# Cross attention by heads, placed between the halves of the query projection's tiles

## The chip, the cores and the metric

The kernel runs on one core of a Trainium2 chip. The metric is device time in microseconds (us) for one execution of the whole program. The kernel before the change takes 1310.12 us (median of three runs, 1309.95 to 1310.24).

Engines are named as in the profile: PE is TensorE (matmuls; PEld are its weight loads), ACT is ScalarE, DVE is VectorE, POOL is GpSimd, SP is SyncE, which issues the DMAs.

## The reference

Two transformer blocks in a row on 512 tokens of width 1024, all in float32. The part that the change touches is the first block's cross attention to a memory of 256 rows, with 4 heads of 256:

```python
def memory_cross_attention(x, mem, wq, wkv, wo):
    q = (x @ wq).reshape(B, S, XA_HEADS, XA_HEAD_DIM)          # S = 512, 4 heads of 256
    k, v = jnp.split(mem @ wkv, 2, axis=-1)                    # M = 256
    ...
    logits = jnp.einsum('bshd,bmhd->bhsm', q, k) * (XA_HEAD_DIM ** -0.5)
    p = jax.nn.softmax(logits, axis=-1)
    o = jnp.einsum('bhsm,bmhd->bshd', p, v).reshape(B, S, D_MODEL)
    return o @ wo
```

Ahead of it stand a mixer (an mLSTM and a sliding-window attention) with a layer norm, and behind it a layer norm, a convolutional feed-forward, and the second block (four mixers, a projection, an MLP).

## The kernel before

**Precision.** Every large product is made of three products of split floats: weights and activations are each held as a high part (`whi`, `xh`) and a low part (`wlo`, `xl`), and PE multiplies high by high, high by low and low by high (L1097 to L1099 where the weights are the stationary operand, L1206 to L1211 where the activations are). The weights come as chunks of 128 x 1024 by DMA into a ring of three `stage` buffers. For each chunk the step `split` casts it on ACT (L1455) and subtracts on DVE (L1870) into a ring of six `whi`/`wlo` buffers. The small products of the attentions are plain float32 matmuls, each shown as two records.

**Order of work.** The class `Plan` writes one list of steps by hand. Each engine walks through this list and executes, in this order, the steps for which it has a function of that name; between engines there are only semaphores. Each engine's own queue is strict. PSUM has eight banks of 128 x 512; `fill` takes the bank that was released first and `out` puts it back with the semaphore value that makes it free. `pump` adds splits so that six chunks are ahead of the one in use.

**Query projection.** `cross_attention` runs `feat("xq", 8)`: eight tiles of 128 features x 512 tokens, 24 matmuls each. Tiles 0 to 3 have their first 256 tokens done already at the end of the layer norm before (`half`), so that only `feat_rest` with 256 tokens is left. ACT copies every tile, scaled by 1/16, into `qT` (L1623).

**Attention, by token tiles of 128.** For token tile i, with all four heads: PE makes the scores of two heads at a time into one bank (`xa_score`, L1365, after all eight query tiles are out); DVE takes the negated row maximum (L2130); ACT makes exp and the row sums into `Lx` (L1632); DVE takes reciprocals (L2135) and multiplies the 128 x 1024 tile (`xa_norm`, L2137); PE turns it in two banks (`xa_turn`, L1373), and ACT copies them into `PTx` (L1637). `Lx` has two buffers. The order is scores 0, scores 1, turn 0, scores 2, turn 1, scores 3, turn 2, turn 3. Then come `decay`, a chain of small operations on parameters of the second block (DVE L2144 to L2171, ACT L1641), and the value product: eight feature tiles k of 512 tokens (`xa_pv`, L1381), each split by ACT (L1646) and DVE (L2175) into `xh` and `xl`, which the output projection "xo" reads.

**An existing helper.** `feat_mid(name, n, mid)` is like `feat`, but cuts each tile's 24 matmuls into a front and a back half and calls `mid()` between them; it does not do so for a tile of which only `feat_rest` is left (but for "in2_a"). The mixers use it: a generator such as `beside_mixer_one` is advanced by one `yield` at each call of `mid`.

Of the kernel before, what the change touches and what calls it, by code (L numbers as in the profile page):

```python
# [47 lines left out]
class Plan:  # L48
# [482 lines left out]

    def cross_attention(self):
        for k in self.feat("xq", 8):
            self.step("xq", k)
            self.out(("xq", k), "q_out", k + 1)

        def scores(i):
            for hp in range(2):
                self.fill("xa_score", i, hp)
                self.step("xa_score", i, hp)  # L540
                self.out(("xa_score", i, hp), "xa_e", 4 * i + 2 * hp + 2)
            self.step("xa_norm", i)

        scores(0)
        for i in range(4):
            if i < 3:
                scores(i + 1)
            for m in range(2):
                self.fill("xa_turn", i, m)
                self.step("xa_turn", i, m)  # L550
                self.out(("xa_turn", i, m), "xa_pt", 2 * i + m + 1)
        self.step("decay")
        for k in range(8):
            self.fill("xa_pv", k)
            self.step("xa_pv", k)
            self.x_split("xo", k)
            self.out(("xa_pv", k), "x_lo", self.x)
        self.step("rows", "ln2")
        self.tok_full("xo", 8, 8)
        self.step("warm", 1)  # L560
        self.boundary("xo", 8, lambda t: self.norm("xo", 1, t))
# [359 lines left out]
def build_program(nc, d, out):  # L921
    plan = Plan()
    with ExitStack() as ctx:
# [26 lines left out]
        def tiles(view, n):  # L950
            return view.rearrange("p (k c) -> p k c", k=n)
# [105 lines left out]
        def tok(t):  # L1057
            return slice(t * 128, (t + 1) * 128)
# [23 lines left out]
        def _(e):  # L1082
            q = Waits(e)

            def fill(*key):

                b, left = plan.bank[key]
                if left:
                    q.wait_ge(S[left[0]], left[1])
                return bank[b]  # L1090
# [267 lines left out]
            def xa_score(i, hp):  # L1358
                b = tiles(fill("xa_score", i, hp)[:], 2)
                q.wait_ge(S["q_out"], 8)  # L1360
                q.wait_ge(S["kt_out"], 8)
                for hh in range(2):
                    h = 2 * hp + hh
                    for kk in range(2):
                        last = e.matmul(b[:, hh, :], qT[:, 2 * h + kk, tok(i)], KT[:, 2 * h + kk, :], start=(kk == 0),  # L1365
                                        stop=(kk == 1))
                last.then_inc(S["xa_s_full"])

            def xa_turn(i, m):
                b = fill("xa_turn", i, m)  # L1370
                q.wait_ge(S["xa_p"], i + 1)
                for h in range(4):
                    last = e.transpose(b[:, tok(h)], Lx[i % 2][:, h, tok(m)], ident[:])  # L1373
                last.then_inc(S["xa_t_full"])

            def xa_pv(k):
                b = fill("xa_pv", k)
                q.wait_ge(S["xa_pt"], 8)
                q.wait_ge(S["vm_out"], 4)
                for m in range(2):  # L1380
                    last = e.matmul(b[:], VM[:, m, tok(k)], PTx[:, m, k // 2, :], start=(m == 0), stop=(m == 1))  # L1381
                last.then_inc(S["xa_o_full"])
# [63 lines left out]
        def _(e):  # L1446
# [178 lines left out]
            def xa_score(i, hp):  # L1625
                b = tiles(bank_of("xa_score", i, hp)[:], 2)
                if i >= 2:
                    q.wait_ge(S["xa_t_full"], 2 * i - 2)
                q.wait_ge(S["xa_m"], 2 * i + hp + 1)
                for hh in range(2):  # L1630
                    h = 2 * hp + hh
                    e.activation(Lx[i % 2][:, h, :], b[:, hh, :], ACT.Exp, bias=lx(i, 1)[:, h:h + 1],  # L1632
                                 accum_out=lx(i, 2)[:, h:h + 1]).then_inc(S["xa_e"])

            def xa_turn(i, m):
                q.wait_ge(S["xa_t_full"], 2 * i + m + 1)
                e.copy(PTx[:, m, :, tok(i)], tiles(bank_of("xa_turn", i, m)[:], 4)).then_inc(S["xa_pt"])  # L1637
# [201 lines left out]
            def m1(k):  # L1839
# [6 lines left out]
                        warm=warm, layer_norm=layer_norm, xq=xq, xa_score=xa_score, xa_turn=xa_turn, decay=decay,  # L1846
# [10 lines left out]
        def _(e):  # L1857
# [270 lines left out]
            def xa_score(i, hp):  # L2128
                q.wait_ge(S["xa_s_full"], 2 * i + hp + 1)
                e.tensor_reduce(lx(i, 1)[:, 2 * hp:2 * hp + 2], tiles(bank_of("xa_score", i, hp)[:], 2), AX.X, ALU.max,  # L2130
                                negate=True).then_inc(S["xa_m"])

            def xa_norm(i):
                q.wait_ge(S["xa_e"], 4 * i + 4)
                e.reciprocal(lx(i, 0), lx(i, 2)).then_inc(own.inc())  # L2135
                after()
                e.tensor_tensor(Lx[i % 2], Lx[i % 2],  # L2137
                                lx(i, 0).rearrange("p (h c) -> p h c", c=1).to_broadcast([128, 4, 256]), ALU.mult
                                ).then_inc(S["xa_p"])
# [474 lines left out]
```

## Time and profile before

| | us |
|---|---|
| median of three runs | 1310.12 |
| the profiled execution | 1310.3 |
| its span | 1308.5 |
| PE busy | 1289.0 |
| DVE busy | 721.7 |
| ACT busy | 556.5 |

The span is the time from the first to the last recorded instruction; the rest of the execution's own time lies around it. The busy times of the engines overlap. In a timeline each row gives start and length in us, the engine, the line of the kernel, the operation, its operands and the number of instructions merged into the row; the brackets give idle time of the engine before the row and what ended it. Starts of consecutive matmuls are closer together than their lengths, since they are pipelined and their ends are modelled.

### The profile page before, as it was taken

The page shows a single profiled execution, that of the slowest core. Times are in us where ns is not written, and L with a number is a line of the kernel's source. Part 1 is how long each engine was busy: PE and PEld are TensorE (multiplying, and loading weights), DVE is VectorE, ACT ScalarE, POOL GpSimd, SP SyncE. Part 2 cuts the span into 40 slices and gives each one's busy share as a digit, 9 for nine tenths or more (in the row PEclk, how much of TensorE's full clock was granted, in tenths as well). Part 3 has the DMA queues.
Part 4 walks back from the last instruction along what each step waited for, and adds up shares of the span by engine and source line. Part 5 has one row for each costly group of instructions (what it writes and reads, how often), then busy time and mean ns, then how long its engine had stood idle before and what let it go on. Part 6 is the DMA issues. An engine that isn't in the chain of part 4 may idle for free.

```text
span 1308.5 us, 16066 instructions
## 1 busy us (share of the span) xinstructions
PE 1289.0 (99%) x6504; PEld 1074.8 (82%) x6504; DVE 721.7 (55%) x1060; ACT 556.5 (43%) x944; POOL 7.0 (1%) x8
## 2 busy tenths in 40 slices
PE   8999999999899999999999989999999999999998
PEld 8877898898589888888888889777898888888886
DVE  5757678563457655555633478877473333433333
ACT  4567644144315544444422354576332422322221
POOL 0000001000000000000000000000000000000000
PEclk9999999999899999999999999999999999999999
DMA  8322245333013333333433123222243233333311
GB/s 271 117 80 65 97 129 160 129 126 117 1 49 104 115 99 97 98 97 100 145 97 97 49 89 125 81 66 88 73 136 95 92 103 98 118 97 100 95 51 65
DMA packets 37714, 131.22 MB, mean 100 GB/s; under 512 B 4324, under 2 KB 5092, under 8 KB 37384
## 3 DMA queue, kind: packets, MB, share of 16 engines
q1 hardware_dynamic: 37640, 130.19, 31.7%
q8 instruction: 52, 0.85, 0.3%
q14 instruction: 22, 0.18, 0.0%
HBM read 128.07 MB, written 2.10 MB: 99 GB/s over the span
## 4 chain that ended last, share of the span: by engine, by line
PE 96%; DVE 1%; ACT 1%; issue 0%; DMA 0%; DVEq 0%; ACTq 0%
PE bank L1097 17%; PE bank L1098 17%; PE bank L1099 17%; PE bank L1206 5%; PE bank L1207 5%; PE bank L1210 5%; PE bank L1209 5%; PE bank L1208 5%; PE bank L1211 5%; PE bank L1381 1%; PE bank L1271 1%; PE bank L1137 1%; PE bank L1148 1%; PE bank L1142 1%; PE bank L1348 1%; PE bank L1334 1%
## 5 line engine op out<-in xcount | busy, mean ns | idle before, releaser
L1097 PE MATMUL bank<-xh,whi 128*128 128x512 f32 (+1 forms) x1168 | 421.8, 361 | 4.1 <-DVE wlo L1870 4.1
L1870 DVE TENSOR_TENSOR wlo<-stage,whi 128x1024 fp32r<-128x1024 f32 (+1 forms) x223 | 268.4, 1209 | 276.0 <-ACT whi L1455 275.8
L1098 PE MATMUL bank<-xl,whi 128*128 128x512 f32 (+1 forms) x1168 | 415.7, 356 | 0.0
L1099 PE MATMUL bank<-xh,wlo 128*128 128x512 f32 (+1 forms) x1168 | 415.5, 356 | 0.0
L1455 ACT CAST whi<-stage 128x1024 fp32r<-128x1024 f32 (+1 forms) x223 | 229.4, 1034 | 216.1 <-PE bank L1211 170.0
L1097 PEld LDWEIGHTS bank<-xh,whi 128*128 128x128 f32 x1168 | 220.6, 189 | 43.2 <-issue 9.3
L1099 PEld LDWEIGHTS bank<-xh,wlo 128*128 128x128 f32 x1168 | 220.6, 189 | 31.5
L1098 PEld LDWEIGHTS bank<-xl,whi 128*128 128x128 f32 x1168 | 220.8, 189 | 30.9 <-issue 0.7
L1206 PE MATMUL bank<-whi,xh 128*128 128x512 f32 x287 | 113.0, 394 | 0.2
L1208 PE MATMUL bank<-wlo,xh 128*128 128x512 f32 x287 | 111.7, 389 | 0.0
L1207 PE MATMUL bank<-whi,xh 128*128 128x512 f32 x287 | 111.7, 389 | 0.0
L1211 PE MATMUL bank<-whi,xl 128*128 128x512 f32 x287 | 111.7, 389 | 0.0
L1209 PE MATMUL bank<-wlo,xh 128*128 128x512 f32 x287 | 111.7, 389 | 0.0
L1210 PE MATMUL bank<-whi,xl 128*128 128x512 f32 x287 | 111.7, 389 | 0.0
L2378 DVE TENSOR_TENSOR R<-bank,R 128x512 f32<-128x512 f32 x32 | 22.1, 692 | 90.5 <-ACT R L1841 90.5
L1841 ACT ACTIVATE R<-bank 128x512 f32<-128x512 f32 x32 | 19.1, 598 | 112.8 <-PE bank L1099 112.8
L2189 DVE SCALAR_TENSOR_TENSOR R<-R,par 128x512 f32<-128x512 f32 x44 | 33.1, 751 | 60.3 <-ACT R L1657 60.3
L1206 PEld LDWEIGHTS bank<-whi,xh 128*128 128x128 f32 x287 | 53.9, 188 | 12.1 <-issue 1.3
L1209 PEld LDWEIGHTS bank<-wlo,xh 128*128 128x128 f32 x287 | 53.9, 188 | 11.3
L1211 PEld LDWEIGHTS bank<-whi,xl 128*128 128x128 f32 x287 | 53.9, 188 | 11.3
L1208 PEld LDWEIGHTS bank<-wlo,xh 128*128 128x128 f32 x287 | 53.9, 188 | 11.3
L1210 PEld LDWEIGHTS bank<-whi,xl 128*128 128x128 f32 x287 | 53.9, 188 | 11.1
(311 smaller groups left out, 1310.1 us busy)
## 6 DMA issues: line engine op xcount, KB each, us to landing
stage<-in_W_m SPq DMA_DIRECT2D x64, 512.0 KB, 3.6
stage<-in_W_up SPq DMA_DIRECT2D x44, 512.0 KB, 3.6
stage<-in_W_down SPq DMA_DIRECT2D x22, 512.0 KB, 3.6
stage<-in_W_in_a SPq DMA_DIRECT2D x19, 512.0 KB, 3.7
stage<-in_W_out SPq DMA_DIRECT2D x16, 512.0 KB, 3.7
stage<-in_W_in_b SPq DMA_DIRECT2D x10, 512.0 KB, 3.7
stage<-in_W_kv_k SPq DMA_DIRECT2D x8, 512.0 KB, 3.6
stage<-in_W_kv_v SPq DMA_DIRECT2D x8, 512.0 KB, 4.1
```

The lines of the kernel that those rows point to most:

```text
L1097: e.matmul(b[:, cols], hi[:, k, :], xh[:, k, cols], start=(k == 0), stop=False)
L1098: e.matmul(b[:, cols], hi[:, k, :], xl[:, k, cols], start=False, stop=False)
L1099: last = e.matmul(b[:, cols], lo[:, k, :], xh[:, k, cols], start=False, stop=(k == 7))
L1206: e.matmul(b[0][:], a_hi, hi[:, 0:512], start=(k == 0), stop=False)
L1207: e.matmul(b[1][:], a_hi, hi[:, 512:1024], start=(k == 0), stop=False)
L1208: e.matmul(b[0][:], a_hi, lo[:, 0:512], start=False, stop=False)
L1209: e.matmul(b[1][:], a_hi, lo[:, 512:1024], start=False, stop=False)
L1210: e.matmul(b[0][:], a_lo, hi[:, 0:512], start=False, stop=end)
L1211: return e.matmul(b[1][:], a_lo, hi[:, 512:1024], start=False, stop=end)
L1455: e.copy(whi[:, i % NSPLIT, 0:width(i)], stage[:, s, 0:width(i)]).then_inc(S["w_hi"])
L1870: e.tensor_tensor(wlo[:, i % NSPLIT, c], stage[:, i % NSTAGE, c], whi[:, i % NSPLIT, c].bitcast(F32), ALU.subtract).then_inc(S["w_lo"])
L2189: e.scalar_tensor_tensor(out=y, in0=u[:, 0:512], scalar=P("fcw", w), in1=y, op0=ALU.mult, op1=ALU.add).then_inc(own.inc())
```

## The change

The attention is cut by heads. For head h, with all four token tiles: `xa_score(h)` makes the scores in two banks of two token tiles, as soon as the query tiles 2h and 2h+1 are out; `xa_exp(h)`, a step of its own now, makes the four exponentials; `xa_norm(h)` multiplies; `xa_turn(h)` turns the four token tiles of this head in two banks, whose copies each fill one whole row of `PTx`; `xa_pv(k)` waits only for its own head k // 2.

The order is a generator, `beside_queries`, advanced by `feat_mid` in the middle of query tiles 4 to 7 and after each of the eight tiles. What is left of it when the queries are done follows then. `decay` moves behind the last `xa_pv`.

```diff
             self.out((name, 2 * t + hf), "ln_z", 8 * s + 2 * t + hf + 1)
 
+    def xa_score(self, h):
+        for z in range(2):
+            self.fill("xa_score", h, z)
+            self.out(("xa_score", h, z), "xa_e", 4 * h + 2 * z + 2)
+        self.step("xa_score", h)
+
+    def xa_turn(self, h):
+        for m in range(2):
+            self.fill("xa_turn", h, m)
+            self.out(("xa_turn", h, m), "xa_pt", 2 * h + m + 1)
+        self.step("xa_turn", h)
+
+    def xa_pv(self, k):
+        self.fill("xa_pv", k)
+        self.step("xa_pv", k)
+        self.x_split("xo", k)
+        self.out(("xa_pv", k), "x_lo", self.x)
+
+    def beside_queries(self):
+
+
+        yield
+        yield
+
+        self.xa_score(0)
+        yield
+
+        self.step("xa_exp", 0)
+        yield
+
+        self.step("xa_norm", 0)
+        self.xa_score(1)
+        yield
+        self.step("xa_exp", 1)
+        yield
+
+        self.xa_turn(0)
+        yield
+        self.step("xa_norm", 1)
+        yield
+
+        self.xa_score(2)
+        yield
+        self.xa_turn(1)
+        self.step("xa_exp", 2)
+        yield
+
+        self.step("xa_norm", 2)
+        yield
+        yield
+        self.xa_pv(0)
+        self.xa_score(3)
+        self.step("xa_exp", 3)
+        self.xa_turn(2)
+        self.step("xa_norm", 3)
+        self.xa_pv(1)
+        self.xa_pv(2)
+        self.xa_pv(3)
+        self.xa_turn(3)
+        self.xa_pv(4)
+        self.xa_pv(5)
+        self.xa_pv(6)
+        self.xa_pv(7)
+        self.step("decay")
+
     def cross_attention(self):
-        for k in self.feat("xq", 8):
+        side = self.beside_queries()
+
+        def mid():
+            next(side, None)
+
+        for k in self.feat_mid("xq", 8, mid):
             self.step("xq", k)
             self.out(("xq", k), "q_out", k + 1)
-
-        def scores(i):
-            for hp in range(2):
-                self.fill("xa_score", i, hp)
-                self.step("xa_score", i, hp)
-                self.out(("xa_score", i, hp), "xa_e", 4 * i + 2 * hp + 2)
-            self.step("xa_norm", i)
-
-        scores(0)
-        for i in range(4):
-            if i < 3:
-                scores(i + 1)
-            for m in range(2):
-                self.fill("xa_turn", i, m)
-                self.step("xa_turn", i, m)
-                self.out(("xa_turn", i, m), "xa_pt", 2 * i + m + 1)
-        self.step("decay")
-        for k in range(8):
-            self.fill("xa_pv", k)
-            self.step("xa_pv", k)
-            self.x_split("xo", k)
-            self.out(("xa_pv", k), "x_lo", self.x)
+            mid()
+        for _ in side:
+            pass
         self.step("rows", "ln2")
         self.tok_full("xo", 8, 8)
...
-            def xa_score(i, hp):
-                b = tiles(fill("xa_score", i, hp)[:], 2)
-                q.wait_ge(S["q_out"], 8)
+            def xa_score(h):
+                q.wait_ge(S["q_out"], 2 * h + 2)
                 q.wait_ge(S["kt_out"], 8)
-                for hh in range(2):
-                    h = 2 * hp + hh
-                    for kk in range(2):
-                        last = e.matmul(b[:, hh, :], qT[:, 2 * h + kk, tok(i)], KT[:, 2 * h + kk, :], start=(kk == 0),
-                                        stop=(kk == 1))
-                last.then_inc(S["xa_s_full"])
-
-            def xa_turn(i, m):
-                b = fill("xa_turn", i, m)
-                q.wait_ge(S["xa_p"], i + 1)
-                for h in range(4):
-                    last = e.transpose(b[:, tok(h)], Lx[i % 2][:, h, tok(m)], ident[:])
-                last.then_inc(S["xa_t_full"])
+                for z in range(2):
+                    b = tiles(fill("xa_score", h, z)[:], 2)
+                    for i in range(2):
+                        for kk in range(2):
+                            last = e.matmul(b[:, i, :], qT[:, 2 * h + kk, tok(2 * z + i)], KT[:, 2 * h + kk, :],
+                                            start=(kk == 0), stop=(kk == 1))
+                    last.then_inc(S["xa_s_full"])
+
+            def xa_turn(h):
+                q.wait_ge(S["xa_p"], h + 1)
+                for m in range(2):
+                    b = fill("xa_turn", h, m)
+                    for i in range(4):
+                        last = e.transpose(b[:, tok(i)], Lx[h % 2][:, i, tok(m)], ident[:])
+                    last.then_inc(S["xa_t_full"])
 
             def xa_pv(k):
                 b = fill("xa_pv", k)
-                q.wait_ge(S["xa_pt"], 8)
+                h = k // 2
+                q.wait_ge(S["xa_pt"], 2 * h + 2)
                 q.wait_ge(S["vm_out"], 4)
                 for m in range(2):
-                    last = e.matmul(b[:], VM[:, m, tok(k)], PTx[:, m, k // 2, :], start=(m == 0), stop=(m == 1))
+                    last = e.matmul(b[:], VM[:, m, tok(k)], PTx[:, m, h, :], start=(m == 0), stop=(m == 1))
                 last.then_inc(S["xa_o_full"])
...
-            def xa_score(i, hp):
-                b = tiles(bank_of("xa_score", i, hp)[:], 2)
-                if i >= 2:
-                    q.wait_ge(S["xa_t_full"], 2 * i - 2)
-                q.wait_ge(S["xa_m"], 2 * i + hp + 1)
-                for hh in range(2):
-                    h = 2 * hp + hh
-                    e.activation(Lx[i % 2][:, h, :], b[:, hh, :], ACT.Exp, bias=lx(i, 1)[:, h:h + 1],
-                                 accum_out=lx(i, 2)[:, h:h + 1]).then_inc(S["xa_e"])
-
-            def xa_turn(i, m):
-                q.wait_ge(S["xa_t_full"], 2 * i + m + 1)
-                e.copy(PTx[:, m, :, tok(i)], tiles(bank_of("xa_turn", i, m)[:], 4)).then_inc(S["xa_pt"])
+            def xa_exp(h):
+                if h >= 2:
+                    q.wait_ge(S["xa_t_full"], 2 * h - 2)
+                for z in range(2):
+                    b = tiles(bank_of("xa_score", h, z)[:], 2)
+                    q.wait_ge(S["xa_m"], 2 * h + z + 1)
+                    for i in range(2):
+                        t = 2 * z + i
+                        e.activation(Lx[h % 2][:, t, :], b[:, i, :], ACT.Exp, bias=lx(h, 1)[:, t:t + 1],
+                                     accum_out=lx(h, 2)[:, t:t + 1]).then_inc(S["xa_e"])
+
+            def xa_turn(h):
+                for m in range(2):
+                    q.wait_ge(S["xa_t_full"], 2 * h + m + 1)
+                    e.copy(PTx[:, m, h, :], bank_of("xa_turn", h, m)[:]).then_inc(S["xa_pt"])
```

The counts of instructions and the names of the semaphores stay; the DVE functions `xa_score(h)` and `xa_norm(h)` have the same change of index (token tile to head) as those shown.

## Rows read from the trace of the kernel before

**Rows 1.** The page: busy time, the clock in 40 slices.

```profile
PE 1289.0 (99%) x6504; PEld 1074.8 (82%) x6504; DVE 721.7 (55%) x1060; ACT 556.5 (43%) x944; POOL 7.0 (1%) x8
...
PEclk9999999999899999999999999999999999999999
```

**Rows 2.** Windows: length, busy PE, PEld, DVE, ACT, POOL, granted clock, DMA.

```profile
280.00:314.00 34.00, 33.52 (x194) 29.41 (x193) 8.93 (x8) 11.19 (x15) 0.00 (x0) 1.00 0.41 136
328.00:330.00 2.00, 2.00 (x11) 1.71 (x10) 1.89 (x3) 0.86 (x3) 0.00 (x0) 1.00 0.00 0
332.00:334.00 2.00, 0.42 (x3) 0.45 (x4) 1.84 (x7) 0.93 (x2) 0.00 (x0) 0.93 0.00 0
334.00:336.00 2.00, 1.39 (x7) 0.99 (x5) 0.00 (x0) 1.16 (x3) 0.00 (x0) 0.50 0.00 0
...
340.00:342.00 2.00, 2.00 (x5) 0.77 (x5) 1.53 (x7) 0.54 (x1) 0.00 (x0) 0.86 0.00 0
```

**Rows 3.** Timeline of PE in the stage: start, duration, line, operands, count, idle before.

```profile
312.45 0.39 PE L1099 MATMUL bank<-xh,wlo 128*128 128x512 f32 x1
...
313.13 0.39 PE L1099 MATMUL bank<-xh,wlo 128*128 128x512 f32 x1
314.30 7.14 PE L1365 MATMUL bank<-R 128*128 128x256 f32 x32 [0.78 <-ACT R L1623]
321.30 1.09 PE L1373 MATMUL bank<-ident,R 128*128 128x128 f32 x8
...
325.68 1.04 PE L1373 MATMUL bank<-ident,R 128*128 128x128 f32 x8
326.56 3.62 PE L1365 MATMUL bank<-R 128*128 128x256 f32 x16
330.01 1.04 PE L1373 MATMUL bank<-ident,R 128*128 128x128 f32 x8
333.58 1.82 PE L1373 MATMUL bank<-ident,R 128*128 128x128 f32 x8 [2.53 <-DVE R L2137]
336.16 16.15 PE L1381 MATMUL bank<-R 128*128 128x512 f32 x32 [0.77 <-ACT R L1637]
...
352.38 0.39 PE L1207 MATMUL bank<-whi,xh 128*128 128x512 f32 x1
```

**Rows 4.** Timeline of ACT in the stage.

```profile
313.55 0.60 ACT L1623 ACTIVATE R<-bank 128x512 f32<-128x512 f32 x1 [3.91 <-PE bank L1099]
...
335.43 0.59 ACT L1637 COPY R<-bank 128x512 f32<-128x512 f32 x1 [0.27 <-PE bank L1373]
...
342.05 0.59 ACT L1646 CAST xh<-bank 128x512 fp32r<-128x512 f32 x1 [1.51 <-PE bank L1381]
...
352.35 0.59 ACT L1646 CAST xh<-bank 128x512 fp32r<-128x512 f32 x1 [1.13 <-PE bank L1381]
```

**Rows 5.** Groups of ACT from 290 to 345: count, busy us, mean ns, idle before.

```profile
L1632 ACT ACTIVATE R<-bank,st 128x256 f32<-128x256 f32 x16 | 7.4, 471 | 5.7 <-DVE st L2130 5.7
...
L1632 ACT ACT_TABLE_LOAD x1 | 1.3, 1283 | 0.0
```

**Rows 6.** Timeline of DVE at the last score and in decay.

```profile
332.21 1.22 DVE L2137 TENSOR_TENSOR R<-R,st 128x1024 f32<-128x1024 f32 x1
...
340.94 0.17 DVE L2171 TENSOR_SCALAR par<-par 128x2 f32<-128x2 f32 x1
```

**Rows 7.** Timeline of PE at two groups between split-float matmuls.

```profile
197.00 2.32 PE L1334 MATMUL bank<-R 128*128 128x512 f32 x8
198.97 0.59 PE L1185 MATMUL bank<-whi,xh 128*128 128x512 f32 x1
199.40 0.40 PE L1186 MATMUL bank<-wlo,xh 128*128 128x512 f32 x1
...
276.31 1.04 PE L1271 MATMUL bank<-ident,R 128*128 128x128 f32 x8
...
277.30 0.28 PE L1098 MATMUL bank<-xl,whi 128*128 128x256 f32 x1
```

More of the change, by code:

```diff
@@ L1845, in _ @@
                         conv_qk=conv_qk, silu_qk=silu_qk, in_o=in_o, ml_exp=ml_exp, kv_k=kv_k, kv_v=kv_v,
-                        warm=warm, layer_norm=layer_norm, xq=xq, xa_score=xa_score, xa_turn=xa_turn, decay=decay,
+                        warm=warm, layer_norm=layer_norm, xq=xq, xa_exp=xa_exp, xa_turn=xa_turn, decay=decay,
                         xa_pv=xa_pv, up=up, rms_stats=rms_stats, rms_late=rms_late, ln_apply=ln_apply, last_norm=last_norm, cf_in=cf_in, cf_first=cf_first, cf_mean=cf_mean,
@@ L2126, in ln_apply, with xa_score, xa_norm @@
                                        op1=ALU.add).then_inc(S["ln_x"])
[L2128 to L2135, printed above, removed]
+            def xa_score(h):
+                for z in range(2):
+                    q.wait_ge(S["xa_s_full"], 2 * h + z + 1)
+                    e.tensor_reduce(lx(h, 1)[:, 2 * z:2 * z + 2], tiles(bank_of("xa_score", h, z)[:], 2), AX.X, ALU.max,
+                                    negate=True).then_inc(S["xa_m"])
+            def xa_norm(h):
+                q.wait_ge(S["xa_e"], 4 * h + 4)
+                e.reciprocal(lx(h, 0), lx(h, 2)).then_inc(own.inc())
                 after()
-                e.tensor_tensor(Lx[i % 2], Lx[i % 2],
-                                lx(i, 0).rearrange("p (h c) -> p h c", c=1).to_broadcast([128, 4, 256]), ALU.mult
+                e.tensor_tensor(Lx[h % 2], Lx[h % 2],
+                                lx(h, 0).rearrange("p (t c) -> p t c", c=1).to_broadcast([128, 4, 256]), ALU.mult
                                 ).then_inc(S["xa_p"])
```

## The prediction

> **What bounds the kernel now.** I read the page's busy table and clock line first [rows 1]. TensorE (PE) is busy for 1289.0 of 1308.5 us, 99%. So a stage is worth only what PE loses in it. The clock line has one digit under 9, at about 335 us. The windows of that place [rows 2] show the granted clock at 1.00 (2.4 GHz) in 328 to 330 and at 0.50 (1.2 GHz) in 334 to 336. Read as shares of the two levels, 0.93 in 332 to 334 puts the fall at 333.7, and 0.86 in 340 to 342 the return at 340.6. That place is the cross attention.
>
> PE's own order of work [rows 3] gives the stage. The queries' matmuls step every 0.227 us (313.13 - 312.45 for three), the last starting at 313.13, so the next could start at 313.36. The first matmul of the output projection that runs in step starts at 352.38, which puts the end of attention at 352.15. The stage takes 352.15 - 313.36 = 38.79 us.
>
> What would it take without waits, at 2.4 GHz? Sixteen score records take 330.01 - 326.56 = 3.45 us, and there are four such groups: 13.80. Eight transposes take 326.56 - 325.68 = 0.88, four groups: 3.52. Once the clock is back, the value product's tiles reach ScalarE (ACT) every (352.35 - 342.05) / 6 = 1.717 us [rows 4]; eight: 13.73. The sum is 31.05, so 7.74 us are lost, as follows.
> - 0.94: the scores wait for ACT's copy of the last query tile (313.36 to 314.30).
> - 0.10: the first 32 score records take 7.00 and not 6.90.
> - 2.69: the last group of turns could start at 330.89 and starts at 333.58. Behind the last score stands a chain: maximum on VectorE (DVE), two exponentials on ACT, reciprocal and product on DVE [rows 6]. From the last score to the first transpose it takes 333.58 - 330.01 = 3.57.
> - 1.70: most of these transposes run at 1.2 GHz, and the value product waits for ACT's second copy of them (started 335.43 [rows 4]); 336.16 instead of 334.46.
> - 2.26: the value product takes 352.15 - 336.16 = 15.99 instead of 13.73, since it runs at 1.2 GHz until 340.6: half of 4.4 us.
>
> **The change part by part.** *Amount of work.* By heads or by token tiles, PE has the same 32 score products of 256 columns, 32 transposes and 16 value products of 512 columns; ACT has the same 16 exponentials and 8 copies, DVE the same 8 maxima and 4 products of 1024. The copy of the turned tile now writes a row in one piece instead of four; the one of before takes 0.59 us [rows 4] and PSUM is read the same, so I cost it at nothing. No DMA is added or moved.
>
> *Places.* The query tiles 0 to 3 run as second halves of 256 columns, without a middle; tiles 4 to 7 have one. That gives 4 + 8 = 12 places for the 12 pieces of the new generator, which fit exactly: scores of head 0 after tile 2; of head 1 and 2 in the middle of tiles 4 and 6; turns of head 0 in the middle of 5, of head 1 after 6. Only pv 0, scores 3, turns 2, pv 1 to 3, turns 3 and pv 4 to 7 come after the queries.
>
> *The switch between kinds of matmul.* This is new: three score groups and two turn groups now stand between the split-float matmuls, and each could cost PE something. In mixer one a group of such products already stands so [rows 7]: from 197.00 to the second split-float matmul at 199.40 is 2.40 us; its 1280 columns at the score's rate (3.45 / 2048 per column) are 2.16, and one step is 0.227: 0.02 is left. Eight transposes between halves: 277.30 - 276.31 - 0.12 = 0.87, the 0.88 of the stage. The other end: if the long step after the group (199.40 - 198.97 = 0.43) were a cost by itself and not the group's own last columns, it would be 0.20. So 5 x 0 to 5 x 0.20; I take 0.2 for all five, near the whole-group figures, which count every column.
>
> *The waits of PE, one by one*, with T the end of tile 7. Scores of head h need tiles 2h and 2h+1 on ACT. ACT starts such a copy 0.2 us after the tile and takes 0.60 [rows 4]; scores 0 to 2 have a tile or a half tile (2.72 us) between. Scores 3 follow T directly, but pv 0 stands before them: 1.72 against about 0.85, 0.87 spare. Turns 0 need the chain from scores 0: I get product 0 done some 4 us before they are reached (the wait in it is DVE's subtraction of a weight chunk, queued before it); turns 1 have over 8 us. Turns 2, reached at T + 5.17, need product 2, which stands after the exponentials 2 and one weight chunk, about T + 1.4: 3.8 spare. Turns 3 are the tight ones. Scores 3 end at T + 1.72 + 3.45 = T + 5.17; by the 3.57 of the chain the transposes could start at T + 8.74. PE has turns 2 (0.88) and pv 1 to 3 (5.15) until T + 11.20: 2.46 spare. Behind turns 3 queue pv 4 to 7 and the whole output projection. pv 6 needs their copies (about T + 13.1) and is reached at T + 15.5. Banks go round in the order of release; I followed them through and each fill finds its bank free by over a microsecond.
>
> *The cover.* What was in the open must fit on ACT and DVE beside the queries and the weight splits. From 280 to 314 ACT is busy for 11.2 of 34 us and DVE for 8.9 [rows 2]. Until T come three heads' exponentials (12 at 0.47 [rows 5]), two pairs of copies (1.1 each) and the table load (1.28): about 9; DVE gets six maxima (about 0.7) and three products of 1.22 with a reciprocal each [rows 6]: about 8.3. Neither passes two thirds, and weight chunks are split six ahead. If this cover fails, the first to show it would be turns 3, one for one after its 2.46 us.
>
> *Decay.* Its chain of small DVE operations ran from the last product's end at 333.43 to 341.11 [rows 6], 7.7 us; it now stands behind pv 7's subtraction, beside the output projection, and ends at most 9.7 us into it. Behind it on DVE is the split of the next weight chunk, which waits for the projection's first chunk (24 steps, 5.4 us) and ACT's cast. It may be late by some 3 us; that chunk is the projection's seventh, used after three whole chunks and three quarters of a chunk, 20.4 us in. SyncE's queue issues the later weights a little later by the same amount; nothing.
>
> *The clock.* With no wait of PE over a microsecond left, nothing resembles what came before the fall at 333.7 (0.94, then 2.69 us idle). So 1.00 throughout.
>
> *Sum.* The new stage is 31.05 + 0.2 = 31.25; 38.79 - 31.25 = 7.54. I keep 0.15 back for small delays at semaphores: gain 7.4. The profiled execution took 1310.3 us (span 1308.5); it becomes 1302.9. The median of the three runs is 1310.12, 0.18 below, so the forecast is 1302.7.
>
> **The rivals.** (a) *Some of it leaks.* At the eight insertions or in the tail small waits stay, 0.1 to 0.5 each, because ACT's copy of a query tile comes behind exponentials, or because each return from the queries' copy to the exponentials loads the table again (1.28). For it: ACT and DVE are strict queues, and three kinds of work now meet there. Against it: the sixteen exponentials of before, with copies of turned tiles between them, have one load in all [rows 5], and the groups in mixer one start without idle time before them [rows 7]. Eight times 0.35: 1305.5.
> (b) *The wait moves to turns 3.* A chain of 3.57 would have to become over 8 us, as it must pass the weight split of ACT and DVE and pv 0's copies first. Then 2.69 idle and the half clock behind it come back, and only the 0.94, the 0.10 and the 0.8 inside 1.70 are won, less 0.2: 1310.1 - 1.6 = 1308.5, which is no change by the bound below. Against it: those passages end before scores 3 do.
> (c) *The clock falls inside the queries; slower than before.* Place: the groups of transposes between halves. If they ended the full clock, PE would run at 1.2 GHz for as long after each as it did here, 6.9 us, which costs half of that, 3.4. Four groups: 13.7, against 7.4 won: 1310.1 + 6.3 = 1316.4. It decides from the third such fall. Against it: the transposes at 325.68 are followed by scores at full rate [rows 3], with the windows of 328 to 330 at 1.00 [rows 2].
> The Trainium skill bears on (c): "TensorE: Matmul & The Clock Gate", Part 4 on transposes, says that the full clock does not engage for the transpose mode. By that rule alone (c) would be likely, and the time 1316.4. The trace disagrees for groups of eight: the clock stays, and they take 0.88 us at 1.00 against 1.82 at 0.50.
> (d) *It doesn't do what it says.* The generator is drained after the queries too, so pieces that found no place would run there with today's waits: 1310. The count of 12 places excludes it.
>
> **How the numbers follow.** Forecast 80%, (a) 12%, (b) 4%, (c) 3%, (d) 1%. The forecast's own spread is 1302.3 (switches free, nothing kept back) to 1303.5 (switches at 1.0). The range reaches into (a): 1302.0 to 1305.6. A difference under 0.2% (2.6 us) is what a measurement here can't tell from none. Faster: forecast and (a), 92%; same: (b) and (d), 5%; slower: 3%.
>
> **What would show it.** In the profile after: the clock line without a low digit; one query tile's distance 5.44 us plus the group in it (8.9 with scores, 6.3 with turns); the output projection's first step near 344.7 instead of 352.15; turns 3 without idle time before them, their product on DVE ending about 2 us earlier; decay beside the projection. Wrong would be: idle time of PE before a score or turn group, a second table load, or a granted clock under 1.00 anywhere between 280 and 350 us.

## The result, and the profile after

The changed kernel takes 1304.4 us (median of four runs, 1301.88 to 1304.76) against 1310.18 for the kernel before: ratio 0.9949, 95% interval 0.9936 to 0.9961. The forecast was 1302.7, in a range of 1302.0 to 1305.6. On a second chip the same kernel took 1302.69 against 1310.33 (first experiment below). The profiled execution took 1304.55 us, its span 1302.8.

The page of the kernel after, its busy table and clock line, which answer to [rows 1]:

```profile
PE 1287.3 (99%) x6504; PEld 1075.6 (83%) x6504; DVE 721.6 (55%) x1060; ACT 556.1 (43%) x944; POOL 7.0 (1%) x8
...
PEclk9999999999999999999999999999999999999999
```

The digit under 9 at 335 us is gone. (A digit is the mean of a fortieth of the span, 32.6 us, so a shorter fall need not show in it; one stands below.) The windows (length, busy PE, PEld, DVE, ACT, POOL, granted clock, DMA) answer to [rows 2] in their first lines:

```profile
280.00:314.00 34.00, 34.00 (x205) 30.68 (x205) 13.30 (x15) 15.20 (x31) 0.00 (x0) 1.00 0.37 109
334.00:336.00 2.00, 2.00 (x6) 0.84 (x5) 1.29 (x2) 0.89 (x3) 0.00 (x0) 1.00 0.56 221
766.00:768.00 2.00, 0.18 (x2) 0.00 (x0) 0.75 (x1) 2.00 (x4) 0.00 (x0) 1.00 0.00 0
768.00:770.00 2.00, 1.47 (x8) 1.47 (x9) 1.96 (x5) 1.06 (x2) 0.00 (x0) 0.76 0.44 47
770.00:772.00 2.00, 2.00 (x11) 2.00 (x11) 2.00 (x2) 0.00 (x0) 0.00 (x0) 0.50 0.54 215
772.00:774.00 2.00, 2.00 (x18) 2.00 (x18) 0.20 (x1) 0.32 (x1) 0.00 (x0) 0.89 0.40 98
```

From 280 to 314 ACT is busy for 15.2 us and not 11.2, DVE for 13.3 and not 8.9: the exponentials and products of heads 0 and 1 and the copies of head 0's turns lie in this stretch (head 2's exponentials follow at 321.32, still ahead of the end of tile 7), and PE is busy for all 34.0. At 334 the clock is at 1.00. But the last four lines show something that the profile of the kernel before does not: PE is almost idle from 766 to 768.5, and the clock is at 0.50 (1.2 GHz) right behind it. The timeline of PE (start, length, line, operands, count, idle time before) answers to [rows 3] and [rows 7]:

```profile
289.18 3.62 PE L1416 MATMUL bank<-R 128*128 128x256 f32 x16
292.45 0.47 PE L1148 MATMUL bank<-xh,whi 128*128 128x256 f32 x1
292.75 0.28 PE L1149 MATMUL bank<-xl,whi 128*128 128x256 f32 x1
...
307.17 1.03 PE L1425 MATMUL bank<-ident,R 128*128 128x128 f32 x8
...
308.27 0.40 PE L1149 MATMUL bank<-xl,whi 128*128 128x512 f32 x1
...
326.01 1.88 PE L1434 MATMUL bank<-R 128*128 128x512 f32 x4
327.73 3.62 PE L1416 MATMUL bank<-R 128*128 128x256 f32 x16
331.18 1.04 PE L1425 MATMUL bank<-ident,R 128*128 128x128 f32 x8
...
337.21 1.04 PE L1425 MATMUL bank<-ident,R 128*128 128x128 f32 x8
...
345.19 0.40 PE L1258 MATMUL bank<-whi,xh 128*128 128x512 f32 x1
```

No row of the stage has idle time before it. Tile 7 ends at 326.01 (T), the last turns start at 337.21, which is the forecast T + 11.20, and the projection is in step at 345.19, so attention ends at 344.96. To compare the stages whatever came before them, I take the start of query tile 3 or of the group placed before it: 288.69 in the kernel before, 289.18 here. From there to the end of attention it was 352.15 - 288.69 = 63.46 us and is 344.96 - 289.18 = 55.78: 7.68 won, 7.54 by the sum, 7.4 in the forecast.

The spans differ by 5.7. The other 2.0 are 0.49 lost before the stage and 1.5 lost behind it. For the second, this is PE at the wait for the fourth weight chunk of the second block's projection, before:

```profile
775.72 0.39 PE L1097 MATMUL bank<-xh,whi 128*128 128x256 f32 x1 [2.35 <-DVE wlo L1870]
...
776.18 0.29 PE L1097 MATMUL bank<-xh,whi 128*128 128x256 f32 x1
776.30 0.28 PE L1098 MATMUL bank<-xl,whi 128*128 128x256 f32 x1
```

and after:

```profile
768.53 0.39 PE L1148 MATMUL bank<-xh,whi 128*128 128x256 f32 x1 [2.35 <-DVE wlo L1925]
...
769.15 0.42 PE L1149 MATMUL bank<-xl,whi 128*128 128x256 f32 x1
769.37 0.41 PE L1150 MATMUL bank<-xh,wlo 128*128 128x256 f32 x1
```

The wait is the same, 2.35 us for the same DVE subtraction. Before, the matmuls of 256 columns go on at 0.12 us apart; after, at 0.21. The window behind the wait shows the full clock before:

```profile
776.00:778.00 2.00, 2.00 (x19) 2.00 (x19) 1.97 (x4) 0.25 (x1) 0.00 (x0) 1.00 0.60 193
```

The first matmul behind the wait starts 7.19 earlier than before, those behind the slow stretch 5.7. The 0.49 comes from the start of the kernel, where the first eight matmuls take 2.3 us to the next ones in all three profiles shown now. Here are before, after, and a third kernel (the experiment "filler"), each in one line:

```profile
9.53 1.35 PE L1148 MATMUL bank<-whi,xl 128*128 128x264 f32 x8
```

```profile
9.59 2.12 PE L1199 MATMUL bank<-whi,xl 128*128 128x264 f32 x8
```

```profile
9.09 1.34 PE L1203 MATMUL bank<-whi,xl 128*128 128x264 f32 x8
```

Before and in "filler" this third group is at its later pace already; after, it takes 2.12 us. The kernels are equal here, so it is the execution that differs. The clock column of the windows reads 1.00 here, but this is no evidence: the profile's clock record begins only at 9.46 us before, 11.27 after and 8.54 in "filler", at the full clock, and that is where each changes its pace. So the slow start fits the half clock, and no row shows it as such. By the fourth group the kernel after is 0.83 behind; up to 33.5 us its groups then start 1.18 us apart against 1.20 before, which gives 0.34 back. Why they do stays open.

### The profile page after: what moved, and what is told of

Same layout as the page of the kernel before. It is cut to its first block, busy times and chain, and to the rows that moved or that the text cites. A ratio compares the mean times of both kernels' runs of the same rounds, so it can differ in the third digit from the quotient of the medians.

```text
span 1302.8 us, 16066 instructions
## 1 busy us (share of the span) xinstructions
PE 1287.3 (99%) x6504; PEld 1075.6 (83%) x6504; DVE 721.6 (55%) x1060; ACT 556.1 (43%) x944; POOL 7.0 (1%) x8
## 4 chain that ended last, share of the span: by engine, by line
PE 98%; DVE 1%; ACT 1%; issue 0%; DMA 0%; DVEq 0%; ACTq 0%
PE bank L1148 18%; PE bank L1149 17%; PE bank L1150 17%; PE bank L1257 5%; PE bank L1259 5%; PE bank L1262 5%; PE bank L1258 5%; PE bank L1260 5%; PE bank L1261 5%; PE bank L1416 1%; PE bank L1434 1%; PE bank L1322 1%; PE bank L1188 1%; PE bank L1199 1%; PE bank L1193 1%; PE bank L1399 1%
## 5 line engine op out<-in xcount | busy, mean ns | idle before, releaser
L1259 PEld LDWEIGHTS bank<-wlo,xh 128*128 128x128 f32 x287 | 53.9, 188 | 11.2
L1260 PEld LDWEIGHTS bank<-wlo,xh 128*128 128x128 f32 x287 | 53.9, 188 | 11.2
L1262 PEld LDWEIGHTS bank<-whi,xl 128*128 128x128 f32 x287 | 53.9, 188 | 11.2
```

Of the source, the lines that this page charges most:

```text
L1259: e.matmul(b[0][:], a_hi, lo[:, 0:512], start=False, stop=False)
L1260: e.matmul(b[1][:], a_hi, lo[:, 512:1024], start=False, stop=False)
L1262: return e.matmul(b[1][:], a_lo, hi[:, 512:1024], start=False, stop=end)
```

## The experiments

All times are medians; the kernel before ran beside each of them on the same chip. T1 is my theory, T2 the rival, as in the expectations.

**The changed kernel again.** No edit.

> The changed kernel once more, to see how its times spread. Theory (T1): the attention stage always wins about 7.7 us; at 766 us TensorE waits 2.35 us for a weight chunk, and whether the clock falls behind that wait differs from execution to execution, so times fall into groups: 1304.3 to 1304.8 with the fall, about 1302 without, the first more often. Rival (T2): something in the new kernel always costs 1.5 us after the stage, then all runs lie within 0.5 us of 1304.5 and the one at 1301.9 was chance.

Measured: 1302.69 us (1302.21 to 1303.77, five runs) against 1310.33: ratio 0.9939 (0.9926 to 0.9953). The profiled run, at 1303.77 the slowest, has the fall again, behind the same wait. The spread is there, T2's fixed 1304.5 is not. The times alone do not form the two clear groups of T1, but the mean granted clock, which is on record for each run, parts them. In the thirteen profiled executions of this document it is 0.999 or 1.000 where the clock falls nowhere ahead of the last microseconds (eight of them), 0.998 in the three with one short fall like this one, and 0.997 in the two with the longer fall of [rows 2]. By it four of the nine timed runs of the changed kernel have a fall: three of the first four, at 1304.25 to 1304.76, and the slowest here, at 1303.77. The other five have 0.999 or 1.000 and take 1301.88 to 1302.95.

```profile
766.00:768.00 2.00, 0.19 (x1) 0.19 (x2) 1.47 (x2) 2.00 (x4) 0.00 (x0) 0.92 0.00 0
768.00:770.00 2.00, 2.00 (x10) 2.00 (x11) 1.97 (x4) 0.34 (x1) 0.00 (x0) 0.50 0.55 160
770.00:772.00 2.00, 2.00 (x15) 2.00 (x15) 1.48 (x2) 0.00 (x0) 0.00 (x0) 0.73 0.25 102
```

**The same order by heads, nothing beside the queries ("drain").**

```diff
-        for k in self.feat_mid("xq", 8, mid):
+        for k in self.feat("xq", 8):
             self.step("xq", k)
             self.out(("xq", k), "q_out", k + 1)
-            mid()
```

> By heads, but nothing placed beside the queries: all pieces follow after query tile 7, in the same order. If the placement brings the gain (T2), the stage is near the 38.8 us of before and the time near 1310. If the order by heads brings it, since value products of finished heads stand where TensorE waited for the last turns (T1), only the 0.94 us wait for the last query copy comes back and perhaps 0.2 at the first turns: stage 31.9 to 32.4 us, clock 1.00, time 0.5 to 1.2 us above the changed kernel where both have or both lack the fall at 770.

Measured: 1304.32 (1302.73 to 1305.02) against 1310.33, ratio 0.9952 (0.9939 to 0.9964). PE's timeline after the queries:

```profile
312.90 7.07 PE L1415 MATMUL bank<-R 128*128 128x256 f32 x32
320.40 1.09 PE L1424 MATMUL bank<-ident,R 128*128 128x128 f32 x8 [0.44 <-DVE R L2192]
...
336.86 1.04 PE L1424 MATMUL bank<-ident,R 128*128 128x128 f32 x8
...
344.83 0.39 PE L1257 MATMUL bank<-whi,xh 128*128 128x512 f32 x1
```

The stage takes 344.60 - 312.90 = 31.70 us; without its 0.44 of idle time at the first turns it would be where the changed kernel is. The 0.94 wait that I had expected here is gone too: the scores of head 0 need only tiles 0 and 1. So T2 falls: of 7.68 us, 7.1 come with the order by heads. In time the kernel lies further above the changed one than the 0.5 to 1.2 expected: 1.6 by the medians, and 1.2 to 1.4 where both have or both lack the fall by their mean clock. By the stages 0.6 of it is explained: 31.70 against 55.78 less 24.67 us for five query tiles, 31.11, in the changed kernel.

**Value products behind the last turns ("turn_first").**

```diff
+        self.xa_turn(3)
         self.xa_pv(1)
         self.xa_pv(2)
         self.xa_pv(3)
-        self.xa_turn(3)
```

> The changed kernel with value products 1 to 3 moved from ahead of the last turns to behind them; the places beside the queries stay. T1 (the order by heads is what hides the last softmax, because these 5.15 us of products stand in front of the last turns): TensorE reaches the turns 0.88 us after the last scores, the chain needs 3.6, so a wait of 2.5 to 2.8 us comes back at the turns, with or without a fall of the clock behind it: 2.7 us above the changed kernel without, 4.4 to 6 with. T2 (the placement beside the queries hides it): under 0.5 us above.

Measured: 1307.13 (1306.21 to 1309.29) against 1310.71, ratio 0.9975 (0.9965 to 0.9984). On the scale of ratios that is 3.4 to 4.7 us above the changed kernel (0.9949 and 0.9939), at the low end of or below the 4.4 to 6 expected with a fall; the mean clock, 0.998 or 0.997, says that all ten runs have at least one. Its PE and its windows:

```profile
334.37 1.37 PE L1425 MATMUL bank<-ident,R 128*128 128x128 f32 x8 [2.43 <-DVE R L2193]
```

```profile
334.00:336.00 2.00, 1.63 (x9) 1.51 (x10) 0.31 (x1) 0.81 (x2) 0.00 (x0) 0.76 0.42 170
336.00:338.00 2.00, 2.00 (x3) 0.67 (x2) 0.00 (x0) 0.36 (x1) 0.00 (x0) 0.50 0.00 0
```

The wait is back at the turns with 2.43 us of idle time, though five groups of PE still lie beside the queries (three of scores, two of turns), and the clock falls behind it. What hides the last softmax is the 5.15 us of value products.

**Matmuls in the later wait ("filler").**

```diff
+                if (name, j) == ("in2_c", 3):
+                    old = w_of(CHUNK0[name] + j - 1, 8)[0]
+                    for z in range(18):
+                        e.matmul(bank_of(name, j)[:, 0:256], old[:, z % 8, :], xh[:, z % 8, 0:256], start=True, stop=True)
```

> The changed kernel with 18 more matmuls of 256 columns (0.12 us each, 2.15 in all, their result overwritten) on TensorE in the 2.35 us wait for the fourth weight chunk of the second block's first projection, at 766 us. T1: the wait is filled, the clock stays at 1.00 there, the 1.5 us of half rate go; no other time changes: 1302.7 to 1303.2, with less spread than the changed kernel. T2 (the clock falls for another reason, or the loss lies elsewhere): the fall at 769 stays and the time is 1304.4 or up to 0.3 more.

Measured: 1302.49 (1301.79 to 1303.09) against 1310.33, ratio 0.9939 (0.9926 to 0.9951). Its clock shows no fall at all in the profile; but the kernel without the filler had come to 1302.69 on this chip, so the medians do not show a gain. Its best run is 0.4 below the other's best, its slowest 0.7 below the other's slowest. The mean clocks say why: only one of that kernel's five runs had a fall to lose. They also decide for T1. With the 2.35 us wait in place (the changed kernel, drain and, below, shift) eight of nineteen runs have 0.998; with the order by heads and without this wait (filler, early_split, both_splits, both_again, both_drain) none of twenty-three has.

**The cause of the later wait ("early_split").** The weight split that PE waits for stood behind the last RMS statistics on ACT, which themselves waited 2.82 us for DVE:

```profile
764.74 1.06 ACT L1733 ACTIVATE R<-R 128x1024 f32<-128x1024 f32 x1 [2.82 <-DVE R L2180]
```

```diff
         self.pump(1)
-        norm(3)
-        self.half(name, 1)
+        self.step("ln_apply", 3)
         self.pump(1)
+        self.step("rms_stats", 3)
+        self.half(name, 1)
```

> The changed kernel with the cause of that wait taken away: the split of the fourth weight chunk is placed ahead of the last RMS statistics and not behind them; ScalarE idles 2.8 us there. T1: the 2.35 us wait shrinks to under 0.3 and the clock does not fall: 1304.4 - 2.1 - 1.5 = 1300.8 where the changed kernel has the fall, 1300.3 to 1301.2. Rival: DVE passes the wait on to the last RMS product, and turns 3 then wait: 1302.5 to 1304.

Measured: 1300.85 (1300.14 to 1301.11) against 1310.33, ratio 0.9925 (0.9913 to 0.9937). It is 1.8 below the changed kernel of the same chip, four of whose five runs had no fall to lose, and the spread falls from 1.6 us to 1.0. PE's waits there, the kernel above first:

```profile
PE bank L1148 <- DVE wlo L1925: 4.1, 2, 2.3
```

```profile
PE bank L1149 <- DVE wlo L1926: 1.7, 1, 1.7
PE bank L1323 <- DVE R L2268: 0.4, 1, 0.4
```

Two waits of 4.1 in total become one of 1.7, and 0.4 reach turns 3: about a sixth of the gain ends where the rival said.

**The same edit in the kernel before ("before_split").**

> The kernel before, with only the split of the fourth weight chunk placed ahead of the last RMS statistics. T1: the wait at the second block's first projection and the clock behind it are no part of the change, so the old kernel wins by this edit what the changed one won, 1.9 us (1.3 to 2.5): ratio to before 0.9985. T2 (the change brought that loss with it): 0 to 0.5 us.

Measured: 1308.52 (1305.08 to 1309.4, eleven runs) against 1310.71, ratio 0.998 (0.9971 to 0.9989): 2.2 us by the medians (2.6 by the ratio). The wait belongs to both kernels; T2 falls. Whether the clock falls behind it in the kernel before too is not shown: the one profile there is has no fall at that place, and the waits that the edit takes away in the trace, 2.35 less a new one of 0.4, account for most of the gain. Two of the eleven runs lie apart, 1305.08 and 1305.27, with a mean clock of 0.999 against 0.996 or 0.997 in the other nine, and the first of them is the profiled one. Its PE and its windows in the attention:

```profile
329.39 1.04 PE L1374 MATMUL bank<-ident,R 128*128 128x128 f32 x8
332.95 1.07 PE L1374 MATMUL bank<-ident,R 128*128 128x128 f32 x8 [2.52 <-DVE R L2138]
334.83 13.97 PE L1382 MATMUL bank<-R 128*128 128x512 f32 x32 [0.82 <-ACT R L1638]
...
348.87 0.39 PE L1208 MATMUL bank<-whi,xh 128*128 128x512 f32 x1
```

```profile
332.00:334.00 2.00, 1.05 (x8) 0.86 (x8) 1.25 (x6) 0.68 (x2) 0.00 (x0) 1.00 0.00 0
334.00:336.00 2.00, 1.18 (x4) 0.68 (x4) 0.99 (x6) 0.79 (x3) 0.00 (x0) 1.00 0.00 0
336.00:338.00 2.00, 2.00 (x6) 0.85 (x5) 1.65 (x10) 0.58 (x1) 0.00 (x0) 1.00 0.03 8
```

These are the waits of [rows 3] to 0.05 us, and the clock stays at 1.00. The stage takes 348.64 - 312.73 = 35.91 us, not 38.79. So of the 7.74 us that the attention lost, 4.86 are waits and slow sequences of their own, and 2.88 are the clock, which falls in most executions and not in all. Here `decay` still stands ahead of the value product, which takes 348.64 - 334.83 = 13.81 us against 13.73 for the same tiles in step; so of the gain by the new order at most 0.1 can come from moving `decay`, which no experiment moved by itself.

**Both later waits ("both_splits").** The changed kernel with early_split's edit and this one:

```diff
-        norm(2)
+        self.step("ln_apply", 2)
         self.step("tail", name, nk, 3, "front")
+        self.used += 3
+        self.pump(1)
         self.turn(name, 1)
+        self.step("rms_stats", 2)
         self.step("tail", name, nk, 3, "back")
-        self.used += TAIL[name]
+        self.used += TAIL[name] - 3
         self.pump(1)
         self.step("rms_apply", 2)
-        self.pump(1)
```

> The changed kernel with the early split of the fourth chunk and also the first chunk's split placed ahead of the third RMS statistics, where ScalarE idles 3.6 us. T1: the 1.7 us wait of TensorE at 754 us goes too: 1.2 to 1.7 us below the kernel with the one early split, ratio to before 0.9925 - 0.0012 = 0.991. Rival: DVE, which now splits before the second turns' subtraction, hands the wait on to the second RMS product: under 0.5 us.

Measured: 1298.8 (1298.39 to 1299.53, four runs) against 1310.71, ratio 0.9911 (0.9897 to 0.9924). It is the fastest kernel of this series. By the ratios it lies 1.8 us below early_split, where 1.2 to 1.7 were expected. From 280 to 790 us PE has one wait left:

```profile
PE bank L1325 <- DVE R L2270: 0.2, 1, 0.2
```

**The later work moved by 1.8 us ("shift").** Eight matmuls of 512 columns more in the feed-forward, with their result overwritten.

```diff
+                if (name, j) == ("up", 12):
+                    q.wait_ge(S["w_lo"], i + 1)
+                    old = w_of(i, 8)[0]
+                    for z in range(8):
+                        e.matmul(b[:], old[:, z, :], xh[:, z, :], start=True, stop=True)
```

> The changed kernel with 8 more matmuls of 512 columns (0.227 us each, 1.8 in all, result overwritten) in the thirteenth tile of the feed-forward's first projection. They only move the later work by 1.8 us. If the fall of the clock behind the 2.35 us wait depends on the moment at which the wait comes, this run has it seldomer: 1.8 us less 0.5 to 1.7 above the changed kernel, ratio to before 0.9940 to 0.9950, and its profile may lack the fall. If the length of the wait alone decides, the fall is there and the time is 1.8 above: 0.9953.

Measured: 1305.21 (1304.38 to 1306.14, five runs: 1304.38, 1304.40, 1305.21, 1306.12, 1306.14) against 1310.71, ratio 0.9959 (0.9946 to 0.9973). The profile lacks the fall behind the same wait (2.34 us), so the length of the wait alone does not decide. By the mean clock two of the five runs have a fall, 1306.12 and 1306.14, and three have none. That is no rarer than the four of nine of the changed kernel, so it is not shown that the moment of the wait matters. The runs with a fall lie 1.7 us and those without 2.0 above their like of the changed kernel (on other chips), near the 1.8 of the added matmuls.

```profile
768.00:770.00 2.00, 0.32 (x3) 0.11 (x1) 0.62 (x1) 1.97 (x5) 0.00 (x0) 1.00 0.00 0
770.00:772.00 2.00, 1.34 (x11) 1.34 (x12) 1.96 (x5) 1.20 (x2) 0.00 (x0) 1.00 0.32 37
```

**The three attentions with the later waits gone.** The base is both_splits once more ("both_again"); "both_drain" has drain's edit on it, "both_before" is the kernel before with the same two early splits.

> The changed kernel with both early splits, again, as the base of the next two: 1298.4 to 1299.5, clock at 1.00 after the start.

> The same, but nothing placed beside the queries: all pieces after tile 7 in the same order by heads. With the later waits gone the spread is small and the placement can be read by itself. T1 (the order by heads brings most): 0.4 to 0.8 us above the base, from the 0.44 us wait at the first turns and a little idle time before it. If the placement brought more than its waits show, over 1.5 us above.

> The kernel before (attention by token tiles after the queries), with both early splits, so that only the attention differs from the base. T1: its waits cost 4.4 us in every run and the clock behind them 3.3 us in most: 7.6 us above the base in most runs (1306.3 to 1307) and 4.3 above in a few (1303), the profile showing which.

Measured, against 1310.74 on the same chip: 1298.71 (1298.12 to 1299.23), ratio 0.9908 (0.9894 to 0.9922); 1299.83 (1299.55 to 1300.07), ratio 0.9917 (0.9904 to 0.9931); 1306.64 (1305.57 to 1307.41), ratio 0.9969 (0.9957 to 0.998). The order by heads is worth 6.8 us and the placement 1.1, together 7.9. The 1.1 lies between the 0.4 to 0.8 of T1 and the rival's 1.5. In the traces the placement is 0.6: from the start of the scores or of tile 3, less 24.67 us for five tiles, the stages take 31.11 and 31.71; the two profiled executions differ by 0.65, as the stages do, and the other 0.5 of the medians is not explained. The kernel both_before did not show the few runs at 1303 that I had expected; its mean clocks are all 0.997 or 0.998, and its profile has the fall at 335 to 342.

## Why the prediction was right, and what it missed

- *What bounds the kernel, and the stage's loss.* Right. The five losses listed add up to 7.69 and not 7.74; the missing 0.05 is the first group of turns, which takes 322.23 - 321.30 = 0.93 and not 0.88. The waits' own part and the clock's were added up as one, though; before_split puts them at 4.86 and 2.88.
- *Places and counts.* The twelve pieces lie as forecast: the tile with scores inside is 8.93 us from the next (295.51 to 304.44), the one with turns 6.33 (304.44 to 310.77).
- *The switch between kinds of matmul.* 0.2 was taken, the trace shows none: 292.75 - 289.18 - 0.12 = 3.45 for the scores of head 0, 308.27 - 307.17 - 0.23 = 0.87 for a group of turns, the same as inside the stage of before. Without this 0.2 and the 0.15 kept back the forecast gain would have been 7.75; the stage won 7.68 and not 7.4.
- *The spare time at the last turns.* Right to the digit. Here is DVE at head 3:

```profile
333.16 0.18 DVE L2191 RECIPROCAL st<-st 128x4 f32<-128x4 f32 x1 [1.09 <-ACT R L1686]
333.37 1.23 DVE L2193 TENSOR_TENSOR R<-R,st 128x1024 f32<-128x1024 f32 x1
```

The product ends at 334.60, the transposes could have started 0.15 later, and they start at 337.21: 2.46 spare.
- *The cover and the table.* ACT ran the same sixteen exponentials, at 0.48 instead of 0.47, with one table load, between eight copies of query tiles. Rival (a)'s reload is refuted:

```profile
L1686 ACT ACTIVATE R<-bank,st 128x256 f32<-128x256 f32 x16 | 7.4, 480 | 2.6 <-DVE st L2186 2.6
L1676 ACT ACTIVATE R<-bank 128x512 f32<-128x512 f32 x8 | 4.8, 598 | 27.1 <-PE bank L1150 27.1
...
L1686 ACT ACT_TABLE_LOAD x1 | 1.3, 1283 | 0.0
```

- *Decay.* Cheaper than bounded: it ends at 352.18, 7.2 us into the projection, and the next weight chunk's subtraction starts at 352.09, 0.25 later within the projection than before.
- *Where the cause was placed.* The text was built on the placement beside the queries, and named the value products in front of the last turns only in one term. By drain, turn_first and both_drain the order by heads is 7.1 of the 7.7 us and the placement 0.6.
- *The clock.* This is the term that failed: "With no wait of PE over a microsecond left" and "So 1.00 throughout". Both were right for the stage and not looked at elsewhere: the second block's boundary had waits of 1.72 and 2.35 us before and after. Behind the 2.35 the clock stood in the profile of before and fell in both profiles of the changed kernel, at a cost of 1.5 us. With the 0.49 of the slow start, that is the distance from 1302.7 to 1304.4 but for the stage's extra 0.3. On the second chip, where four of five runs had no fall, the median is 1302.69: the forecast was that of an execution without the fall, how near a median comes to it depends on how many runs have one, and an agreement to 0.01 is luck. Rival (c) priced a fall at 3.4 us; the two kinds measured cost 1.5 and 2.88, neither of them at its place. It counted four groups of transposes where only two stand among the queries. Transposes between halves do no harm: the shown group takes 0.87 us within a stretch whose mean granted clock is 1.00. The Trainium skill ("TensorE: Matmul & The Clock Gate", Part 4) says that the full clock doesn't engage for the transpose mode; the trace differs for groups of eight of them among matmuls.
- *The spread.* The forecast's own 1302.3 to 1303.5 was too narrow on the first chip, whose median lies above it, and right on the second. It held only the unknown costs of the change, and neither the clock's part in other stages nor the slow start.

Whether the new times of the work make that fall more frequent than the old ones stays open, and so does what decides whether the clock falls behind such a wait. The run shifted by 1.8 us settled neither.

## What to carry to other kernels

When a softmax or another serial chain of engines stands before the last group of matmuls, look first for an order in which finished parts leave independent matmuls to put in front of that group; by the traces it brought twelve times what the interleaving with the stage before brought (7.1 against 0.6 us), by the medians six times (6.8 against 1.1). Compare the chain's length with these matmuls' time: here 3.57 against 6.03 us.

Waits of TensorE of 2.35 to 2.53 us cost more here than their length in some executions: the clock fell behind them in five of the ten cases profiled. Behind the 1.72 us wait at the second block's boundary it fell in none of nine. So list the waits of the whole kernel and not only those of the stage, forecast with and without a fall of the clock behind each long one, and remove the others too: each of the two here went by moving one weight split ahead of a step that waited anyway.

## What the runs showed of the hardware that was not expected

- The same wait in the same place, 2.52 us before the last turns, is followed by half a clock in the profile of the kernel before and by the full clock in that of before_split. By their mean clock two of eleven runs were of the second kind, 3.3 us faster.
- The start is slow for a different length from execution to execution: the third group of eight matmuls takes 1.34 to 2.12 us, which moves what stands behind it by up to 1.3 us between executions (scores of head 0 at 289.18 in the profile after and 287.85 in that of "filler").
- With all waits over 0.5 us gone but the first of the kernel ("both_again"), the time scatters by 1.1 us, against 3.9 for the kernel before on the same chip.
